# Two 2-layer blocks on one core: rope's exchange of halves moved to ScalarE, f32 side products made in 16-bit parts, tiles reordered

## The reference

```python
# first block, one layer (twice)
x = x + 0.5 * _swiglu(_rms_norm(x, ffn1_norm[l]), ffn1_w_gu[l], ffn1_w_down[l])
x = x + _hybrid_mixer(_rms_norm(x, mix_norm[l]), ...)
x = x + 0.5 * _swiglu(_rms_norm(x, ffn2_norm[l]), ...)

# _hybrid_mixer: u, va -> gated token mixing; q, k, qi, ki -> rope -> selection of 64 keys, attention
q, k, qi, ki = _rope(...)                       # x1*cos - x2*sin, x2*cos + x1*sin over the two halves of a head
score = einsum('bqhs,bqh->bqs', relu(qi @ ki), wi)
return (gate_a * y_a + gate_b * y_b) @ w_out

# second block, one layer (twice): branches a, b, c, d and a gated merge
q = (rmsnorm(cq, q_norm_g) @ w_uq)              # branch b: latent products, then rope on 32 of 96 features
kv = (rmsnorm(ckv, kv_norm_g) @ w_ukv)
k = concatenate([k_nope, broadcast_to(k_pe, ...)])
hid = gelu(blocks.reshape(B, n_cmp, 32 * 64) @ w1 + b1)   # branch c: compression of 15 blocks, for keys and for values
cmp = hid @ w2 + b2                             # beside it: attention "s" (selected) and "w" (window) with keys ks, kw
merged = sum(sigmoid(h @ w_merge[i] + b_merge[i]) * (y_i @ w_branch[i]) for i in range(4))
x = x + merged @ w_out[l]
```

## Time and profile before

| | |
|---|---|
| median of 3 runs | 1637.09 us |
| the profiled execution | 1634.92 us, its span 1633.1 us |
| TensorE busy | 1607.5 us (98%), 14454 matmul records |
| GpSimd busy | 1000.0 us (61%), 542 instructions |
| VectorE busy | 503.6 us (31%) |
| ScalarE busy | 366.1 us (22%) |
| DMA | 294.93 MB, mean 181 GB/s |

### The profile page before, as it was taken

One profiled execution on the slowest core, in us unless ns is written; L12 is line 12 of the kernel. 1 busy time (PEld: TensorE's weight loads), 2 busy tenths in 40 slices (PEclk: granted clock), 3 DMA queues, 4 the chain that ended last, 5 costly groups with the idle time before them and its releaser, 6 DMA issues.

```text
span 1633.1 us, 32788 instructions
## 1 busy us (share of the span) xinstructions
PE 1607.5 (98%) x14454; PEld 1411.1 (86%) x14454; DVE 503.6 (31%) x1128; ACT 366.1 (22%) x902; POOL 1000.0 (61%) x542
## 2 busy tenths in 40 slices
PE   7999999999999999999999999999999999999998
PEld 6888888888888888888888888888888888788887
DVE  3111264343110211126534311133523233433323
ACT  3111124212110211112421211023333122324212
POOL 6877656666777577765566677745265765346571
PEclk9999999999999999999999999999999999989999
DMA  9556454555555565544555465534444654334451
GB/s 366 201 205 206 144 181 156 181 207 176 196 200 204 194 210 197 202 168 160 175 172 196 177 207 202 195 104 160 148 165 156 207 180 168 134 133 169 167 204 52
DMA packets 42621, 294.93 MB, mean 181 GB/s; under 512 B 4720, under 2 KB 6256, under 8 KB 7792
## 3 DMA queue, kind: packets, MB, share of 16 engines
q1 hardware_dynamic: 42480, 292.84, 51.5%
HBM read 291.78 MB, written 1.05 MB: 179 GB/s over the span
## 4 chain that ended last, share of the span: by engine, by line
PE 95%; DVE 2%; ACT 1%; issue 1%; POOL 0%; DMA 0%; SPq 0%; DVEq 0%; ACTq 0%
PE ps L510 27%; PE ps L511 27%; PE ps L512 27%; PE ps L528 2%; PE ps L530 2%; PE ps L529 1%; PE ps L771 1%; PE ps L607 1%; PE ps L613 1%; PE ps L625 1%; PE ps L599 1%; PE ps L546 1%; DVE diag L1210 1%; PE ps L597 1%; POOL w_low L486 0%
## 5 line engine op out<-in xcount | busy, mean ns | idle before, releaser
L486 POOL TENSOR_TENSOR w_low<-ring 128x1024 f16<-128x1024 f32 (+2 forms) x538 | 999.8, 1882 | 600.8 <-DMA ring<-in_w 600.6
L510 PE MATMUL ps<-hP,ring 128*128 128x256 f16 (+1 forms) x2976 | 812.5, 273 | 2.7 <-ACT work L1123 1.4
L511 PE MATMUL ps<-hP,ring 128*128 128x256 f16 (+1 forms) x2976 | 812.0, 273 | 0.0
L512 PE MATMUL ps<-hP,w_low 128*128 128x256 f16 (+1 forms) x2976 | 812.0, 273 | 0.0
L510 PEld LDWEIGHTS ps<-hP,ring 128*128 128x128 bf16 (+1 forms) x2976 | 292.1, 98 | 47.1 <-issue 7.5
L511 PEld LDWEIGHTS ps<-hP,ring 128*128 128x128 bf16 (+1 forms) x2976 | 292.0, 98 | 34.4
L512 PEld LDWEIGHTS ps<-hP,w_low 128*128 128x128 f16 (+1 forms) x2976 | 291.9, 98 | 33.8
L511 PE MATMUL ps<-work,ring 128*128 128x256 f16 x1088 | 296.7, 273 | 0.0
L510 PE MATMUL ps<-work,ring 128*128 128x256 f16 x1088 | 296.5, 272 | 0.0
L512 PE MATMUL ps<-work,w_low 128*128 128x256 f16 x1088 | 296.3, 272 | 0.0
L1253 DVE TENSOR_TENSOR ps<-work,ps 128x256 f32<-128x256 f32 x88 | 37.8, 429 | 335.7 <-PE ps L512 312.0
(11 more groups left out here) (201 smaller groups left out, 1202.9 us busy)
## 6 DMA issues: line engine op xcount, KB each, us to landing
ring<-in_w SPq DMA_DIRECT2D x268, 1024.0 KB, 4.8
con<-in_const SPq DMA_DIRECT2D x1, 2732.0 KB, 17.1
gm<-in_gm SPq DMA_DIRECT2D x2, 1024.0 KB, 17.1
ring<-in_w SPq DMA_DIRECT2D x2, 640.0 KB, 6.3
ring<-in_w SPq DMA_DIRECT2D x2, 560.0 KB, 4.3
ring<-in_w SPq DMA_DIRECT2D x2, 544.0 KB, 3.5
xT<-in_x SPq DMA_DIRECT2D x4, 256.0 KB, 3.8
out<-work SPq DMA_DIRECT2D x8, 128.0 KB, 2.0
```

Source lines behind the costliest of these rows:

```text
L486: nc.gpsimd.tensor_tensor(w_low[:, c % SLOTS, a:b], ring[:, c % SLOTS, a:b], w_high[:, c % SLOTS, a:b], ALU.subtract).then_inc(split.by((c ...
L510: nc.tensor.matmul(bank, w_high[:, slot, a:a + m], rhs(k, 0), start=(k == 0), stop=False)
L511: nc.tensor.matmul(bank, w_high[:, slot, a:a + m], rhs(k, 1), start=False, stop=False)
L512: mm = nc.tensor.matmul(bank, w_low[:, slot, a:a + m], rhs(k, 0), start=False, stop=(k == kt - 1))
```

## The change

- **Exchange of halves by ScalarE.** `copy_raw` and TensorE's `swap` go. ScalarE copies each group of 32 partitions from the left half of the bank to its partner group in the right half: four copies per tile in A, two per tile in B (and one more for the 64 features of bq that are not turned). VectorE's three operations per tile now follow each other (`rotate`). In B the rope features are laid 32 apart (`apart`), so that rk and bq tiles have 128 rows in place of 96.
- **Latent products and compression in parts.** cq, ckv and the blocks get high and low parts (`cqP`, `ckvP`, `blkP`), and the mla and w1 chunks are split by GpSimd. `parts` issues the three 16-bit products.
- **Shared tiles.** kc is one tile with 64 rows of ks and 64 of kw (before: two tiles, each with its keys twice); cmp is one tile with kc and vc. ScalarE writes each key to both halves; VectorE builds all blocks from the one tile.
- **Order of tiles.** In A the u and va tiles come ahead of the ga tiles. In B: see the list below; kcmp and vcmp come last, and six merge groups stand around the turning of b.
- **Diagonals.** ScalarE makes both halves, in the norms and for the key scale of branch b.
- Small things: `normalise` with a gate puts the reciprocals into PSUM; the masking of w_s moves to the start of mixer A; another rotation of banks for the merges (`PAIR_B`).

```diff
+TILES_B = [("aq", 0), ("aq", 1), ("ak", 0), ("ak", 1), ("cq", 0), ("ckv", 0), ("rk", 0), ("av", 0), ("lat", 0), ("av", 1),
+           ("qc", 0), ("qc", 1), ("kc", 0), ("cvg", 0), ("cvg", 1), ("rkv", 0), ("ag", 0), ("ag", 1), ("cmp", 0), ("cg", 0),
+           ("cg", 1), ("bg", 0), ("bk", 0), ("bk", 1), ("bk", 2), ("bk", 3), ("bv", 0), ("bv", 1), ("bq", 0), ("bq", 1),
+           ("bq", 2), ("bq", 3), ("hid", 0), ("hid", 1), ("bg", 1), ("dq", 0), ("dq", 1), ("dk", 0), ("dk", 1), ("dv", 0),
+           ("dv", 1), ("dg", 0), ("dg", 1), ("kcmp", 0), ("vcmp", 0)]
...
-                    pe.wait_ge(*diag_a.at(s))
-                    nc.tensor.matmul(ps[:, 7, 0:P], ones[:, :], diag[:, 0:P], start=True, stop=True)
-                    pe.wait_ge(*diag_v.at(s))
-                    nc.tensor.matmul(ps[:, 7, P:T], ones[:, :], diag[:, P:T], start=True, stop=True
-                                     ).then_inc(spread.by(s), 1)
+                    for t in range(TT):
+                        pe.wait_ge(*diag_made.at((s, t)))
+                        mm = nc.tensor.matmul(ps[:, 7, t * P:t * P + P], ones[:, :], diag[:, t * P:t * P + P], start=True, stop=True)
+                    mm.then_inc(spread.by(s), 1)
...
-                    turn_pairs("qi", 0), turn_pairs("qi", 1)
                     gemm("wi", 0), gemm("wi", 1)
-                    turn_pairs("qi", 2), turn_pairs("qi", 3)
-                    gemm("q", 0)
-                    turn_pairs("ki", 0)
-                    gemm("q", 1)
-                    turn_pairs("q", 0)
...
+                    def parts(bank, piece, k, at, m, rhs, start, stop, rows=slice(0, P)):
+
+                        c, a = PLACE[piece][k]
+                        a += at
+                        weights(c, a, a + m)
+                        slot = c % SLOTS
+                        nc.tensor.matmul(bank, w_high[rows, slot, a:a + m], rhs(0), start=start, stop=False)
+                        nc.tensor.matmul(bank, w_high[rows, slot, a:a + m], rhs(1), start=False, stop=False)
+                        return nc.tensor.matmul(bank, w_low[rows, slot, a:a + m], rhs(0), start=False, stop=stop)
...
-                            nc.tensor.matmul(ps[0:HD, b, 0:T], ring[:, whole(mla), 768 + n * HD:768 + (n + 1) * HD], ckvT,
-                                             start=True, stop=True).then_inc(done.by(end), 1)
+                            parts(ps[0:HD, b, 0:T], (s, "mla", 0), 0, 1024 + n * HD, HD, lambda part: ckvP[:, 0, part, :],
+                                  True, True).then_inc(done.by(end), 1)
...
-                            nc.tensor.matmul(ps[0:96, b, 0:T], ring[:, slot, a:a + 96], cqT[:, 0, :], start=True, stop=False)
-                            nc.tensor.matmul(ps[0:96, b, 0:T], ring[0:HD, slot, PACK + a:PACK + a + 96], cqT[0:HD, 1, :],
-                                             start=False, stop=True).then_inc(done.by(end), 1)
+                            pe.wait_ge(*taken(s, ("rk", 0)))
+                            parts(ps[:, b, 0:T], (s, "mla", 0), 0, P * n, P, lambda part: cqP[:, 0, part, :], True, False)
+                            parts(ps[:, b, 0:T], (s, "mla", 0), 0, 512 + P * n, P, lambda part: cqP[0:HD, 1, part, :], False, True,
+                                  slice(0, HD)).then_inc(done.by(end), 1)
                         elif kind == "hid":
-                            slot = whole(PLACE[s, "w1", n][0][0])
-                            pe.wait_ge(*taken(s, ("cmp", n)))
+                            pe.wait_ge(*blk_low.at(s))
                             for k in range(16):
-                                mm = nc.tensor.matmul(ps[:, b, 0:NCMP], ring[:, slot, k * P:(k + 1) * P], blk[:, n, k, :],
-                                                      start=(k == 0), stop=(k == 15))
+                                ks = slice(k * NCMP, (k + 1) * NCMP)
+                                mm = parts(ps[:, b, 0:NCMP], (s, "w1", n), k, 0, P, lambda part: blkP[:, n, part, ks], k == 0, k == 15)
                             mm.then_inc(done.by(end), 1)
...
-                    gemm("lat", 0), gemm("ag", 0), gemm("ag", 1), gemm("qc", 0), gemm("rkv", 0), gemm("qc", 1)
+                    gemm("qc", 0), gemm("qc", 1), gemm("kc", 0), gemm("cvg", 0), gemm("cvg", 1), gemm("rkv", 0), gemm("ag", 0)
+                    turn(s, "a")
+                    gemm("ag", 1)
+                    mix(s, "a", lambda t, h: a_v[:, t, h * HD:h * HD + HD])
+                    gemm("cmp", 0)
+                    pe.wait_ge(*y_low.at((s, "a")))
+                    pe.wait_ge(*taken(s, ("kc", 0)))
+                    scores(s, "s", lambda h: head(c_qkT, 0, h), lambda h: half(c_qkT[:, 2, :], h))
+                    gemm("cg", 0), gemm("cg", 1), gemm("bg", 0)
                     for n in range(4):
                         gemm("bk", n)
                     gemm("bv", 0), gemm("bv", 1)
-                    turn(s, "a")
-                    gemm("bq", 0), gemm("bq", 1), gemm("kc", 0)
-                    mix(s, "a", lambda t, h: a_v[:, t, h * HD:h * HD + HD])
-                    turn_pairs("bq", 0)
-                    gemm("bq", 2)
-                    turn_pairs("bq", 1)
-                    gemm("bq", 3), gemm("kc", 1)
-                    turn_pairs("bq", 2), turn_pairs("bq", 3)
-                    pe.wait_ge(*y_low.at((s, "a")))
-                    pe.wait_ge(*taken(s, ("kc", 1)))
-                    scores(s, "s", lambda h: head(c_qkT, 0, h), lambda h: half(c_qkT[:, 2, :], h))
-                    gemm("cvg", 0), gemm("cvg", 1), gemm("cmp", 0), gemm("cmp", 1), gemm("cg", 0)
+                    for n in range(4):
+                        gemm("bq", n)
+                    gemm("hid", 0)
                     turn(s, "s")
-                    gemm("cg", 1)
+                    gemm("hid", 1)
                     mix(s, "s", lambda t, h: c_vg[:, t, 0:HD])
...
-                    nc.scalar.activation(diag[:, 0:P], const("ident"), ACT.Copy, scale=rcol[:, 1, 0:1]
-                                         ).then_inc(diag_a.by(s), 1)
+                    for t in range(TT):
+                        nc.scalar.activation(diag[:, t * P:t * P + P], const("ident"), ACT.Copy, scale=rcol[:, 1, t:t + 1]
+                                             ).then_inc(diag_made.by((s, t)), 1)
...
+                        for q in range(4):
+                            r, o = slice(32 * q, 32 * q + 32), slice(32 * (q ^ 1), 32 * (q ^ 1) + 32)
+                            ins = nc.scalar.activation(ps[r, b, T:2 * T], ps[o, b, 0:T], ACT.Copy)
+                        ins.then_inc(swapped.by((s, kind, n)), 1)
...
+                        if kind == "bq":
+                            nc.scalar.activation(b_qT[0:HD, n, :], ps[0:HD, b, 0:T], ACT.Copy)
+                        nc.scalar.activation(ps[64:96, b, T:2 * T], ps[96:P, b, 0:T], ACT.Copy)
+                        nc.scalar.activation(ps[96:P, b, T:2 * T], ps[64:96, b, 0:T], ACT.Copy
+                                             ).then_inc(swapped.by((s, kind, n)), 1)
...
+                        elif kind == "kc":
+                            for w in range(2):
+                                for o in (0, HD):
+                                    ins = nc.scalar.activation(c_qkT[o:o + HD, 2 + w, :], ps[HD * w:HD * w + HD, b, 0:T], ACT.Copy)
...
+                    act.wait_ge(*taken(s, ("cmp", 0)))
+                    nc.scalar.activation(blkP[:, :, 0, :], blk, ACT.Copy).then_inc(blk_high.by(s), 1)
+                    gate("cg", 0)
+                    exps(s, "s")
+                    gate("cg", 1), gate("bg", 0)
                     take("bv", 0), take("bv", 1)
-                    copy_turned(s, "a")
-                    copy_raw("bq", 0), copy_raw("bq", 1)
-                    take("kc", 0)
-                    y_parts(0)
-                    copy_raw("bq", 2), copy_raw("bq", 3)
-                    take("kc", 1), take("cvg", 0), take("cvg", 1)
-                    exps(s, "s")
-                    gate("cg", 0)
+                    for n in range(4):
+                        swap("bq", n)
...
-                def cosines(s, t, rows, bank, cos, dst):
-                    dve.wait_ge(*raw_copied.at((s,) + t))
-                    nc.vector.tensor_tensor(dst, ps[rows, bank, 0:T], cos, ALU.mult).then_inc(cos_done.by((s,) + t), 1)
-
-                def sines(s, t, rows, bank, sin):
+                def rotate(s, t, rows, bank, cos, sin, product):
+
                     dve.wait_ge(*swapped.at((s,) + t))
+                    nc.vector.tensor_tensor(product, ps[rows, bank, 0:T], cos, ALU.mult).then_inc(cos_done.by((s,) + t), 1)
                     nc.vector.tensor_tensor(ps[rows, bank, T:2 * T], ps[rows, bank, T:2 * T], sin, ALU.mult
                                             ).then_inc(turned_done.by((s,) + t), 1)
+                    dve.wait_ge(*cos_done.at((s,) + t))
...
+                    def latent_low(j, kind, rows, latent):
```

(13 more changed lines are left out.)

469 lines of the change are left out of this document (218 added, 251 removed), and 4 rows, old and new, of the table TILES_B.

## The result

The changed kernel took 1588.24 us, the median of four runs (1587.22 to 1589.62), against 1635.47 us for the kernel before (1631.63 to 1637.34): a ratio of 0.972 with a 95% interval of 0.971 to 0.974. The forecast was 1589, its own range 1583 to 1598. The profiled execution has a span of 1585.4 us in place of 1633.1, 47.7 us less.

A forecast was written before the change was run, and what follows sets the result against it. The prediction took TensorE to bound the kernel, in flight for 98% of the span. Gains of 57.0 us less costs of 11.0 gave net 46 us, from 1634.9 to 1589 us; own range 1583 to 1598, 8 in 10 1577 to 1606.

The forecast's parts named there:

- the compression: B mixers: 32 f32 products per layer become 96 16-bit ones, 19.6 us to 4.9 us, a gain of 14.7 us.
- the clock: B mixers: the granted clock no longer falls to half around the f32 compression, a gain of 4.5 us.
- The B waits: Mixer B: new TensorE waits among short products, 3.6 us per layer, with a merge wait 7.8 us in all.
- The wait before bk 2: Mixer B: bk 2 waits for a bank behind ScalarE's tanh of cg 1, 0.5 us or so.
- The 2.0 us for the last key k 3: A mixers: TensorE reaches the first scores sooner and waits for the last rotated key, 1.0 us per layer.
- GpSimd's split among the waits: Stated sign of being wrong: GpSimd's split appears among TensorE's new waits in B; no cost was charged for it.
- The diagonals: Norms: ScalarE makes the second diagonal too, so TensorE's wait for VectorE shrinks, a net gain of 3.0 us.
- the exchange with its waits: A and B mixers: 36 f32 exchange products go, 15.8 us, and their waits on VectorE, 2.0 us.
- The latent products: Mixer B: products of bk, bv and bq go from 7.7 to 5.3 us per layer, a gain of 4.9 us.
- The charge for the clock falling again: Mixer B: the new thin stretch of waits and short products may lower the clock, a cost of 1.2 us.
- (a): Rival: the new waits do not come, B loses 3 us and A nothing; 1580 us, chance 0.14.
- (e): Rival: ScalarE's exchange is the bound at 1.9 us per copy, kernel slower, 1708 us; chance 0.03.

The follow-up runs named there:

- before_exch_a: The kernel before with only the exchange of halves in the two A mixers made by ScalarE's four copies, orders as before: 1641.97 us, ratio 1.0054 to the kernel before.
- cos_first_a: The changed kernel with VectorE's order in the A mixers as before (products with cos of qi 0 to 3 first): 1597.62 us.
- gate_first: The changed kernel with the gate of bg 0 ahead of the low part of the blocks on VectorE: 1587.18 us.
- bg1_early: The changed kernel with tile bg 1 ahead of bk 0 in mixer B, dq 0 and dq 1 around the mixing of s: 1583.53 us.

## Why the prediction was right

**What held.** The bound was TensorE, and pricing its products by the distance of starts gave the tiles (10.5), the compression (14.7) and the clock (4.5, measured 4.4) to within 0.1 us. The B waits came where they were said to come: before bk 3 (1.6 and 1.5 us, said 1 to 2.5), before the compression (0.46, said 1 to 1.5) and before the mixing (0.82, said 0.3 to 0.6). Stage by stage the stated ranges were met: A 4 to 6 us, B0 14 to 18, B1 17 to 22, FFN 0.5.

**What was off, and cancelled.** The wait before bk 2 did not come. The 2.0 us for the last key k 3 were 0.16 us per mixer: VectorE was done with it at 242.43, the scores began at 242.58. In its stead came 0.6 us per mixer for va 0 and four switches from 16-bit to f32 products of 0.09 us each, which had stood inside the exchanges before. The compressed probabilities of branch c (1.4 and 0.9 us) were not foreseen: I had priced VectorE's stall behind GpSimd at one place, L1520, and not looked for other instructions that work in SBUF alone. The prediction named GpSimd's split among the waits as a sign of being wrong; here it stood behind one, at one remove. The diagonals gave 1.3 us more than said, and the exchange with its waits 1.6 us more. The latent products gave 1.0 us less: they took 7.5 us per layer before, not 7.7, and 5.5 after, not 5.3. The charge for the clock falling again (1.2 us) was not needed. That the sum came within 2 us of the measured difference is in part luck: six terms were off by 0.4 to 1.6 us, in both directions. Rivals (a) to (e) did not happen; (a) came nearest in the A mixers, and (e) was far off: a copy took 0.351 us.

**What the sum did not say.** It booked 17.8 us of gain to the exchange and 1 us per mixer to its consequences, as though the two were a property of the exchange. `before_exch_a` shows that in the A mixers the exchange by itself loses 7 us. That it gains rests on VectorE's order and on the tile order, worth 18.5 us together there. The prediction had this in one half sentence ("two more projection tiles stand ahead of the turning") and gave it no number. The forecast stood because the diff brought both.

**Open.** Why with the old tile order the clock fell in A1 (behind a wait of 3.9 us) but not in A0 (3.5 us), and with the exchange alone in both (3.3 and 2.4 us), no run tells. The same wait at q 0 was followed by a fall in both mixers of `cos_first_a` and in one of `before_exch_a`. The exchange in mixer B, the shared tiles and the latent products were priced from the trace; no run takes one of them back alone.

## What to carry to other kernels

Work taken off the bounding engine brings it sooner to everything that it waits for. Before booking the gain, lay the next engine's unbroken run beside it and count the tiles that cover it; if they don't reach, the gain is gone, and here in most cases the clock with it. And where a wait ends an unbroken run of another engine, reordering that run moved the wait (`gate_first`), while one tile more of cover removed it (`bg1_early`); only the wait for bq 0's own bank stayed.

## What was not expected of the hardware

- A 128 x 8 operation of VectorE between SBUF operands took 1.88 and 1.42 us beside GpSimd's split, until the end of the half in work, 0.17 us behind it, and 0.17 us in PSUM beside it; a reduction from SBUF right ahead of it took 0.28 us, beside the same split.
- TensorE takes 0.09 us extra at each change between 16-bit and f32 products (0.20 us in place of 0.11 from start to start, L512 to L756 in the kernel before), and between 128 and 64 rows or columns of weights (0.20 us in place of 0.11 in bq, L718 to L716).
- ScalarE's copies of 32 x 64 start every 0.133 us, those of 32 x 256 every 0.36 us.
- Ten times in four runs TensorE waited 2.2 to 3.9 us in a mixer A. Behind seven of these waits the granted clock fell to half, for 3.4 us each time; behind three, of 3.5, 2.5 and 2.2 us, it stayed full.
